# Cross-attention of a two-block network on one core: whole heads instead of query blocks, and where the projections stand between them

## What is computed

```python
h = h + memory_cross_attention(rms_norm(h, norm_xattn_g[layer]), mem_n, wq, wkv, wo)   # layer = 0, 1

def memory_cross_attention(xn, mem_n, wq, wkv, wo):      # 4 heads of 256
    q = (xn @ wq).reshape(B, T, 4, 256)
    k, v = the two halves of (mem_n @ wkv), made early in the program for both layers
    s = einsum('bthd,bmhd->bhtm', q, k) * 256 ** -0.5
    p = softmax(s, axis=-1)
    o = einsum('bhtm,bmhd->bthd', p, v).reshape(B, T, 1024)
    return o @ wo
```

## Time and profile before

| | |
|---|---|
| median of three runs | 3285.48 us |
| the profiled execution | 3284.78 us |
| its span, first to last instruction | 3283.0 us |
| TensorE matmul | 3114.7 us busy, 95% |
| VectorE, ScalarE, GpSimd | 1558.8, 1175.8, 126.5 us busy |
| mean granted TensorE clock | 0.98 |

### The profile page before, as it was taken

The page is one execution under the profiler, slowest core; times in us unless marked ns, Lnnn a source line. Parts: engine busy times, 40 slices in busy tenths (PEclk is TensorE's granted clock), DMA queues, the critical chain, the costliest instruction groups (busy, mean ns, idle before and its releaser), DMA issues.

```text
span 3283.0 us, 39941 instructions
## 1 busy us (share of the span) xinstructions
PE 3114.7 (95%) x17208; PEld 2490.4 (76%) x17208; DVE 1558.8 (47%) x1957; ACT 1175.8 (36%) x1564; POOL 126.5 (4%) x142
## 2 busy tenths in 40 slices
PE   8889988799999989899999998899999999999999
PEld 6787766577887766777887785588888887878887
DVE  4444446546544664546544654543335343363333
ACT  4343332434322464344322544532224322342221
POOL 1010000100000100100000200000001000000000
PEclk9899999899999999999999999999999999999999
DMA  4333001213332321313332231033323212133321
GB/s 150 119 131 104 15 21 40 77 52 90 103 90 85 94 64 52 103 42 97 92 97 78 91 90 52 26 94 98 93 87 116 81 64 93 65 103 90 103 90 64
DMA packets 355617, 270.60 MB, mean 82 GB/s; under 512 B 28672, under 2 KB 341504, under 8 KB 355184
## 3 DMA queue, kind: packets, MB, share of 16 engines
q1 hardware_dynamic: 351504, 252.83, 25.8%
q0 software_dynamic: 3936, 15.22, 1.3%
HBM read 261.73 MB, written 6.29 MB: 82 GB/s over the span
## 4 chain that ended last, share of the span: by engine, by line
PE 84%; DVE 8%; ACT 5%; issue 1%; POOL 0%; DMA 0%; DVEq 0%; SPq 0%; ACTq 0%; POOLq 0%
PE ps L189 83%; ACT arena L203 2%; DVE arena L220 2%; ACT whi L206 1%; DVE arena L212 1%; DVE wlo L212 1%; PE ps L192 1%; DVE hT L212 1%; DVE sml L229 1%; DVE xlo L220 1%; DVE arena L216 1%; ACT arena L206 0%; DVE split L212 0%; ACT L203 0%; POOL arena L212 0%
## 5 line engine op out<-in xcount | busy, mean ns | idle before, releaser
L189 PE MATMUL ps<-xhi,whi 128*128 128x512 f32 (+2 forms) x2192 | 874.1, 399 | 12.3 <-DVE wlo L212 4.2
L189 PE MATMUL ps<-xhi,wlo 128*128 128x512 f32 (+2 forms) x2192 | 857.1, 391 | 0.0
L189 PE MATMUL ps<-xlo,whi 128*128 128x512 f32 (+2 forms) x2192 | 856.7, 391 | 0.0
L189 PE MATMUL ps<-split,whi 128*128 128x512 f32 (+2 forms) x2640 | 830.9, 392 | 14.7 <-DVE split L212 10.4
L212 DVE TENSOR_TENSOR wlo<-wraw,whi 128x2048 fp32r<-128x2048 f32 (+4 forms) x258 | 550.7, 2137 | 475.6 <-ACT whi L206 475.4
L189 PEld LDWEIGHTS ps<-split,whi 128*128 128x128 f32 (+1 forms) x2640 | 491.5, 189 | 143.1 <-issue 26.6
L206 ACT ACTIVATE whi<-wraw 128x2048 fp32r<-128x2048 f32 (+4 forms) x258 | 456.2, 1771 | 352.8 <-PE ps L189 342.9
L189 PE MATMUL ps<-split,wlo 128*128 128x512 f32 (+2 forms) x1320 | 509.8, 386 | 0.0
L189 PEld LDWEIGHTS ps<-xhi,whi 128*128 128x128 f32 (+2 forms) x2192 | 410.9, 187 | 119.1 <-issue 10.4
L189 PEld LDWEIGHTS ps<-xhi,wlo 128*128 128x128 f32 (+2 forms) x2192 | 410.5, 187 | 91.9 <-issue 5.9
L189 PEld LDWEIGHTS ps<-xlo,whi 128*128 128x128 f32 (+2 forms) x2192 | 410.3, 187 | 90.6
(11 more groups left out here) (110 smaller groups left out, 2041.3 us busy)
## 6 DMA issues: line engine op xcount, KB each, us to landing
wraw<-in_ffn_w_up SPq DMA_DIRECT2D x128, 512.0 KB, 5.2
wraw<-in_ffn_w_down SPq DMA_DIRECT2D x32, 1024.0 KB, 5.0
wraw<-in_odd_w_in SPq DMA_DIRECT2D x24, 1024.0 KB, 5.2
wraw<-in_ffn_w_gate SPq DMA_DIRECT2D x44, 512.0 KB, 3.9
wraw<-in_xattn_wkv SPq DMA_DIRECT2D x16, 1024.0 KB, 5.6
wraw<-in_xattn_wq SPq DMA_DIRECT2D x8, 1024.0 KB, 5.1
wraw<-in_xattn_wo SPq DMA_DIRECT2D x8, 1024.0 KB, 5.2
wraw<-in_cd_w_in SPq DMA_DIRECT2D x8, 1024.0 KB, 5.6
```

Source lines behind the costliest of these rows:

```text
L189: return self.e.matmul(out, lhsT, rhs, start=start, stop=stop, skip_group_check=True)
```

## The change

- Q0 takes its two banks and the norm's sum from the tuple (0, 1, 2), and the sum is asked for after 6 row tiles in `xattn0` and after 4 in `xattn1`. Q1 comes straight behind Q0, in banks 6 and 7; the other queries use banks 4 to 7 in turn.
- The four workers go. Each step is made for a whole head: scores of four query blocks in two banks (0, 1), maxima of two blocks by one instruction, one scaling and one reciprocal for four, eight transposes in two banks (2, 3), two copies of 512 columns in place of four of 256, output products of 512 columns (four in place of sixteen of 128) in two banks (4, 5), and two high and two low halves of 512 columns.
- The order is written out on each engine. On TensorE query blocks q4 to q7 stand between the parts of heads 0 to 2, and O0 and O1 between those of heads 2 and 3, cut by row tile, in banks 6, 7 and 0, 1. O2 and O3 follow as before.
- On ScalarE `W.round` of O0 stands behind the copy of q5 and that of O1 behind the copy of q7; on VectorE `W.rest` of O0 stands ahead of head 0's `weights`, that of O1 ahead of head 2's.

The diff, with the removed lines left out (they are in the listing above):

```diff
--- before.py
+++ after.py
@@ -506,7 +506,7 @@
                     bs = [ps.take(*key, of=of) for key, _, _ in group]
                     for k in range(u.kts):
                         if early and k == sum_at:
-                            early.sum(pe)
+                            early.sum(pe, of)
                         for (key, m0, m), b in zip(group, bs):
                             pe.wait_ge(early.raw(k) if early else made(k))
                             if k == 0:
@@ -879,58 +879,101 @@
 
         def xattn(l, before, prev, nxt, memory):
 
+
             S = Stage(f"xattn{l}", sem)
             at[0] = 0
             S.carry = carry = Carry(S, *nxt)
             norm = Fresh(S, prev)
             oo = [als() for _ in range(8)]
...
             kv, qq = al(4096), al(4096)
             kk, vv = kv[:, 0:2048], kv[:, 2048:4096]
             l_kv = landing(f"kv{l}")
             units = fm_units("q", 1024, [(D["xattn_wq"][l], 0)])
             out = add_units("out", [P] * 8, D["xattn_wo"][l])
...
+            p, pT = al(1024), al(1024)
+            mx, sm = sml[:, 0:4], sml[:, 4:8]
+            of_s, of_t, of_o = (0, 1), (2, 3), (4, 5)
             ends = before
 
             def tensor(pe):
...
+                for _ in fm_tensor(pe, S, units[0:1], X8, norm.made, of=(0, 1, 2), fresh=norm, sum_at=(6, 4)[l]):
+                    pass
+                name, parts, bn, blocks = units[1]
+                u = W.take(name, parts, bn)
+                bs = [ps.take(*key, of=(6, 7)) for key, _, _ in blocks]
+                for k in range(8):
+                    for (key, m0, m), b in zip(blocks, bs):
+                        pe.wait_ge(W.ready(name), ps.empty(*key), norm.made(k))
+                        i_ = mm3(pe, b, u, k, m0, m0 + m, X8[k], k == 0, k == 7)
+                        if k == 7:
+                            i_.then_inc(*up(S.P, *key, unit=name if key == blocks[-1][0] else None))
+                queries = fm_tensor(pe, S, units[2:], X8, norm.made, of=(4, 5, 6, 7))
+
+                def scores(hd):
+                    for n in range(2):
+                        b = ps.take("s", hd, n, of=of_s)
+                        for i in (2 * n, 2 * n + 1):
+                            pe.wait_ge(S.A.of("q", 2 * hd + 1) if hd else S.V.of("q", 1), l_kv.of("x"), ps.empty("s", hd, n))
+                            for d in range(2):
+                                c = (2 * hd + d) * T + i * P
+                                i_ = pe.mm(b[:, i % 2 * 256:i % 2 * 256 + 256], qq[:, c:c + P],
+                                           kk[:, (2 * hd + d) * 256:(2 * hd + d + 1) * 256], d == 0, d == 1)
+                        i_.then_inc(*up(S.P, "s", hd, n))
+
+                def turn(hd):
+                    bs = [ps.take("turn", hd, j, of=of_t) for j in range(2)]
+                    for j in range(2):
+                        for i in range(4):
+                            pe.wait_ge(S.V.of("p", hd, i), ps.empty("turn", hd, j))
+                            i_ = pe.tr(bs[j][:, i * P:(i + 1) * P], p[:, i * 256 + j * P:i * 256 + (j + 1) * P], ident)
+                        i_.then_inc(*up(S.P, "turn", hd, j))
+
+                def output_of(hd):
+                    for d in range(2):
+                        b = ps.take("o", hd, d, of=of_o)
                         for j in range(2):
...
+                            c = j * 1024 + hd * 256 + d * P
+                            pe.wait_ge(S.A.of("pT", hd, j), ps.empty("o", hd, d))
+                            i_ = pe.mm(b, vv[:, c:c + P], pT[:, j * T:(j + 1) * T], j == 0, j == 1)
+                        i_.then_inc(*up(S.P, "o", hd, d))
+
+                taken = {}
+
+                def rows(n, ks):
+
+                    name, parts, bn, blocks = out[n]
+                    if n not in taken:
+                        taken[n] = W.take(name, parts, bn), [ps.take(*key, of=((6, 7), (0, 1))[n]) for key, _ in blocks]
+                    u, bs = taken[n]
+                    for k in ks:
+                        for (key, m), b in zip(blocks, bs):
+                            pe.wait_ge(W.ready(name), S.V.of("o", k // 2, k % 2), ps.empty(*key))
+                            i_ = mm3(pe, b, u, k, m * P, m * P + P, oo[k], k == 0, k == 7)
+                            if k == 7:
+                                i_.then_inc(*up(S.P, *key, unit=name if key == blocks[-1][0] else None))
+
+                next(queries)
+                scores(0)
+                next(queries)
+                scores(1)
+                turn(0)
+                next(queries)
+                output_of(0)
+                turn(1)
+                scores(2)
+                next(queries)
+                output_of(1)
+                turn(2)
+                scores(3)
+                rows(0, range(0, 4))
+                output_of(2)
+                turn(3)
+                rows(0, range(4, 6))
+                output_of(3)
+                rows(1, range(0, 4))
+                rows(0, range(6, 8))
+                rows(1, range(4, 8))
+                for _ in add_tensor(pe, S, out[2:], oo, [P] * 8, lambda k: S.V.of("o", 3, 1)):
                     pass
 
             def vector(dve):
@@ -946,32 +989,43 @@
 
                 norm.vector(dve, first_queries)
 
...
+                def maxima(hd):
+                    for n in range(2):
+                        dve.wait_ge(S.P.of("s", hd, n), S.V.own())
+                        dve.rmax(mx[:, 2 * n:2 * n + 2], chunks(ps.ap("s", hd, n), 2)).then_inc(*up(S.V))
+                    dve.wait_ge(S.V.own())
+                    dve.ts(mx, mx, -1.0 / 16, None, ALU.mult).then_inc(*up(S.V, "max", hd))
+
+                def weights(hd):
+                    dve.wait_ge(S.A.of("exp", hd, 3))
+                    dve.recip(sm, sm).then_inc(*up(S.V))
+                    dve.wait_ge(S.V.own())
+                    for i in range(4):
+                        w = p[:, i * 256:(i + 1) * 256]
+                        dve.ts(w, w, sm[:, i:i + 1], None, ALU.mult).then_inc(*up(S.V, "p", hd, i))
+
+                def low_half(hd):
+                    for d in range(2):
+                        o = oo[2 * hd + d]
+                        dve.wait_ge(S.A.of("ohi", hd, d))
+                        dve.tt(o.lo, ps.ap("o", hd, d), o.hi.bitcast(F32), ALU.subtract).then_inc(
+                            *up(S.V, "o", hd, d, frees=("o", hd, d)))
+
+                W.rest(dve, units[2][0])
+                maxima(0)
+                W.rest(dve, units[3][0])
+                weights(0)
+                maxima(1)
+                weights(1)
+                low_half(0)
+                maxima(2)
+                W.rest(dve, out[0][0])
+                weights(2)
+                low_half(1)
+                maxima(3)
+                weights(3)
+                low_half(2)
+                low_half(3)
                 for _ in add_vector(dve, S, out, carry):
                     pass
 
@@ -980,41 +1034,50 @@
                 act.wait_ge(*ends())
                 norm.scalar(act, lambda: W.round(act, units[1][0]))
 
...
+                def query(j):
+                    act.wait_ge(S.P.of("q", j))
+                    act.copy(qq[:, j * T:(j + 1) * T], ps.ap("q", j)).then_inc(*up(S.A, "q", j, frees=("q", j)))
+
+                def exps(hd):
+                    for i in range(4):
+                        act.wait_ge(S.V.of("max", hd), S.P.of("turn", hd - 1, 1) if hd else NEVER)
                         act.tables(ACT.Exp)
...
+                        act.act(p[:, i * 256:(i + 1) * 256], ps.ap("s", hd, i // 2)[:, i % 2 * 256:i % 2 * 256 + 256], ACT.Exp,
+                                bias=mx[:, i:i + 1], scale=1.0 / 16, acc=sm[:, i:i + 1]).then_inc(
+                            *up(S.A, "exp", hd, i, frees=("s", hd, i // 2)))
+
+                def turned(hd):
+                    for j in range(2):
+                        act.wait_ge(S.P.of("turn", hd, j), S.P.of("o", hd - 1, 1) if hd else NEVER)
+                        act.copy(pT[:, j * T:(j + 1) * T], ps.ap("turn", hd, j)).then_inc(
+                            *up(S.A, "pT", hd, j, frees=("turn", hd, j)))
+
+                def high_half(hd):
+                    for d in range(2):
+                        act.wait_ge(S.P.of("o", hd, d))
+                        act.copy(oo[2 * hd + d].hi, ps.ap("o", hd, d)).then_inc(*up(S.A, "ohi", hd, d))
+
+                query(2)
+                query(3)
+                W.round(act, units[2][0])
+                query(4)
+                exps(0)
+                query(5)
+                W.round(act, units[3][0])
+                turned(0)
+                exps(1)
+                query(6)
+                high_half(0)
+                turned(1)
+                exps(2)
+                query(7)
+                W.round(act, out[0][0])
+                high_half(1)
+                turned(2)
+                exps(3)
+                high_half(2)
+                turned(3)
```

(36 more changed lines are left out.)

46 lines of the change are left out of this document (removed).

## The result

The changed kernel takes 3279.18 us (median of eight runs, 3274.40 to 3282.28) against 3285.91 us for the kernel before on the same chip (eight runs): **0.9973 of the time, 95% interval 0.9963 to 0.9982**, 8.9 us less. Its profiled execution, 3274.40 us, is the fastest of the eight. On another chip five runs gave 0.9961 (0.9949 to 0.9974). The forecast median was 3274.4 us, 0.9966 of the kernel before; both intervals hold that ratio, and the measured median is 4.8 us above the forecast one.

A forecast was written before the change was run, and what follows sets the result against it. TensorE, busy 95% of the span, was taken as the bound, by its work, waits and slow running. Terms 1.3+3.7+4.2+2.7-0.8 = 11.1 us off 3284.78 gave 3273.7, median 3274.4 us; range for all 3263 to 3284.

The forecast's parts named there:

- Q0 held by its banks: Start of both attention stages: banks read late, so the sum starts at 611.3, not 604.9, and at 1342.6, not 1336.34.
- the signs: Things to see in the changed profile, among them TensorE idle ahead of Q0, about 7 us in xattn0, 4.5 in xattn1.
- the first rival: Start of both stages: the banks don't hold Q0 up, total about 3266 us; chance 0.13.
- Q1 straight behind Q0: Q1 ahead of head 0's scores: 1.3 us gained in xattn0 and 3.7 us in xattn1.
- The attention: From Q1 and head 0's scores to the next stage: 4.2 us gained in xattn0, 2.7 in xattn1.
- the third rival: Attention heads: the gaps only move, heads 1 and 3 wait too, 2.4 us twice a stage; 3284, chance 0.10.
- The low clock behind the short waits: Attention part: 1.5 us for slow matmuls after waits of together 6.1 us in xattn0.
- Elsewhere: mix1: 1.5 us lost ahead of out 0, the 0.78 us wait of block "if" gone; net 0.8 lost.
- The median: Whole kernel: median 0.7 us above the profiled execution's 3273.7, giving 3274.4 us.
- every short wait paid with 2.2 us of low clock: Rival: five waits a stage each cost this, not 0.5 to 1; 3287, or 3281 with half; chance 0.12.
- The slower one: Rival, Q0's restart to head 2's transposes: 3.05 us lost after each of five waits a stage; 3295, chance 0.07.
- the sign "more than 10 us a stage": Both attention stages: the prediction is wrong if windows at clock 0.50 cover more than 10 us a stage.

The follow-up runs named there:

- the run with the scores first: Changed kernel with head 0's scores put ahead of Q1 again, nothing else; 0.9990 of the time of the kernel before.
- the weights-first run: Changed kernel with VectorE scaling head 0's and head 2's weights ahead of the low halves of O0 and O1; 0.9919 of the kernel before.
- The first execution: Profiled execution of the changed kernel on the first chip, nothing further edited: 3274.40 us; that chip's runs gave 0.9973 of the kernel before.
- The second execution: Profiled execution of the unedited changed kernel on another chip, where its runs gave 0.9961 of the kernel before.
- The best version: Changed kernel with Q0's banks free, bank rotation restored behind both attention stages, and weights ahead of O0's and O1's low halves; 3246.22 us, 0.9876 of the kernel before.
- the rotation set on: Changed kernel with the common rotation of the eight banks advanced by 5 after the out units of both attention stages; 0.9934 of the kernel before.
- the filling: Changed kernel plus 20 matmuls whose result nobody reads, put ahead of Q0 in both stages; 0.9965 of the kernel before.

## Why the prediction came out right, and which terms were off

**Q0 held by its banks: right.** The holders are the ones counted: VectorE's additions of out 5 and out 6 end at 600.29 and 602.30, and q0 and q1 start at 600.44 and 602.36. The sum stands where it was forecast: 612.10 less the 0.8 us by which the whole program runs later at A's start is 611.3. The idle time is 4.9 us where the signs said 7, since q0's first row tile already ran in between; that changes nothing in the sum, which went by q1. Freeing the banks gave 8.9 us, the first rival's 8, so that rival is refused in its premise and confirmed in its price.

**Q1 straight behind Q0: right in place.** Q1's fifth row tile was forecast 40.2 us behind A's start and came at 40.0; head 0's transposes at 653.7, from the Q1 end of 633.3, which is 67.1 behind A's start, and they came at 67.0. The stop of 1.11 us ahead of Q1's first tile was not forecast; the later stop swallowed it. The 1.3 and 3.7 us of this part were net of the hold. Taken by itself, Q1's place is worth 6 to 14 us (the run with the scores first) and, in the kernel before, 10 by the ruler and 15 by the ratio. I had not worked out that part apart from the hold, and so never saw that it alone matched the forecast.

**The attention: waits right, two errors that cancel.** Heads 0 and 2 wait in both stages and heads 1 and 3 in neither; the third rival falls. With the crawl behind the scalings, transposes ended 2.4 and 2.5 us late in the first stage where the sum had 2.3 and 2.4; O2's 1.04 was forecast as 1.4 and out 4's 3.38 as 1.4+2.4. What was off is this:

- *The work was priced too long.* The warm prices are a record's duration, where the distance of two starts is what counts. A head's scores cost 3.26 us (665.54 to 668.80), not 3.62, and its transposes 0.88, not 1.04. In the weights-first run the stretch from Q1's end to the next stage has 97.9 us of work, where the sum has 95.6+3.6 = 99.2: 1.3 us too much in each stage.
- *The low clock behind the short waits was mis-sized.* I had it at one fixed 1.5 us a stage, 3.0 in all. The first execution shows none in the first stage (A fell by 8.1 us, not 5.5) and 5.8 in the second, behind head 0's and head 2's transposes and behind out 4 (B should have fallen by 3.7+2.7-1.5 = 4.9 and fell by 1.9). The second execution shows 1.7 and some 3.

So the clock cost 2 to 3 us more than charged, the work 2.6 less, and the total of A+B, 10.4 forecast and 10.0 measured, is as close as it is by luck.

**Elsewhere: right.** 1.53 us lost ahead of out 0, 0.78 gained.

**The median.** "0.7 above the profiled execution" was the kernel before's spread. The changed kernel's eight runs spread over 7.9 us, and the longest has a mean granted clock of 0.978, the shortest 0.981. The forecast of the profiled execution, 3273.7, hit 3274.40, but this was the fastest of the eight. Of the forecast total, 11.1 us, the first chip shows 8.9 and the second 12.8.

**The rivals of the clock.** One had every short wait paid with 2.2 us of low clock. Of the transposes' four waits two were followed by a clock of 1.00 and two by 0.50, at 1.7 us each. The slower one, 21 more, wanted 6.1 us at 0.50 behind each of five waits in both stages, 61 in all; from Q0's restart on the first execution has 10.2 us in the first stage and 20.5 in the second. That is over the sign "more than 10 us a stage", so by this sign the prediction would be wrong. The sign was badly set, for the kernel before has 13.7 and 20.5. The Trainium skill ("TensorE: Matmul & The Clock Gate", section "HAM oscillation — how this bites in real kernels") tells of a kernel that waits 3 to 5 us between bursts and pays the low clock again in each. The trace agrees at Q0's restart in the second stage (4.46 us, then a window at 0.51); behind out 4 (3.4 us) it agrees in one execution and not in the other.

**The gain that didn't come.** The change could have brought about 40 us. It gave some 9 back through Q0's banks, 9 through the rotation's phase (in part the same), and 13 through two low halves in front of the weights, and part of the first by a sum that was asked for late. How much of the 40 is due to whole heads, and how much to the out units that stand between them, no run separates.

## What to carry to other kernels

When a stage is rewritten to take fewer banks from a shared rotation, list who holds each bank that the stage and those behind it take next: a fixed tuple at a stage's start should name the banks that the stage ahead read first. Don't price a wait on TensorE by its idle time alone, nor by a fixed factor: the four waits of 1.8 us gave back almost twice their idle time, the holds of 4.5 to 4.9 us about once. Look for the rest in the work behind the wait. Before rewriting a stage, try its cheapest reorder alone: moving Q1 by two turns brought as much as the whole rewrite.

## What the runs showed of the hardware beyond that

- The same kernel with the same waits ran a window behind a 3.4 us wait at 0.50 in one execution and at 1.00 in another, 2.5 us of B. The best version's four runs spread over 1.5 us and the changed kernel's eight over 7.9, but fewer waits are no surety: with the rotation set on, five runs spread over 12.6.
- Keeping TensorE busy through a hold kept the clock full there, and it then stood at 0.50 longer at the next stop than without: a window of 0.50 in place of 0.72 in the first stage. From Q0's restart on the first stage has 13.7 us at 0.50 either way; the second has 10.2 with the filling and 13.7 without, and ended 0.2 sooner. One execution shows it, in both stages; why wasn't tried.
- Plain float32 output products of 512 columns cost 3.43/8 = 0.43 us a record, with two records for each product. Made 128 columns at a time, the same output cost 3.49 us a head from start to start (655.69 to 659.18 in the kernel before): the wider products alone gain next to nothing.
